# A hybrid decoder step: gate projections of branches D and B ahead of their branch products, kept in DRAM, and two VectorE passes of a triangular inverse in other steps

## Chip, cores and metric

The kernel runs on one core of a Trainium2 chip. The metric is the device time of one execution in microseconds (us), the median of the runs. Engines are named as the profile names them: PE (TensorE matmul), PEld (its weight load), DVE (VectorE), ACT (ScalarE), POOL (GpSimd), SP (SyncE, which here only issues DMAs).

## What is computed

One layer of a decoder for 512 prompt tokens and 8 sample tokens together (520 columns in all). Four branches read one projection of the normed input; each branch output goes through its own matrix and is weighted by a sigmoid gate, and the sum goes on. Cross attention over 256 memory tokens and a convolutional FFN follow. The reference, cut to the part that the change touches:

```python
def token_mixer(xn, p, hist, past):
    z = xn @ p['w_in']
    (a_h, a_b, a_c, g_q, g_k, g_v, g_z, g_a, g_b, c_v, c_g, f_q, f_k, f_v, f_f, gate) = split_cols(z, IN_WIDTHS)
    ...                                            # o_a: short gated conv, o_c: conv + LayerNorm
    o, S = gated_delta_chunked(q, k, v, g_log, beta, hist['gdn'])
    o = rmsnorm(o, p['gdn_norm']) * silu(g_z)      # o_b
    ...
    o_d = forgetting_attention(fq, kk, vv, c[:, -T:], c, q_pos, k_pos)   # the samples: 2048 cached tokens
    gates = sigmoid(gate).reshape(B_, T, N_BRANCH, D_MODEL)
    for i, o_i in enumerate((o_a, o_b, o_c, o_d)):
        merged = merged + gates[:, :, i] * (o_i @ p['w_branch'][i])
    out = merged @ p['w_out']

def gated_delta_chunked(q, k, v, g, beta, s0):     # chunks of C tokens
    A = where(strict, (kb @ k.T) * L, 0) + eye(C)
    sol = triangular_solve(A, concat([v * beta, kb * exp(d)]))
    u, w = sol[..., :DV], sol[..., DV:]
    def step(S, xs):                               # the state goes from chunk to chunk
        v_new = u_i - w_i @ S
        o = qd_i @ S + qk_i @ v_new
        S = S * dl_i + kd_i.T @ v_new
```

## The kernel before

**Pieces.** All large matrix products go through one list, made by `plan`: a *unit* is a block of 256 weight columns, a *piece* is 128 of them, done in two *halves* of 260 tokens. A piece of `w_in` has 8 K tiles, one of `w_branch` 4; each K tile takes three matmuls of 128x260 (high x high, high x low, low x high parts of float32), so a half is 24 or 12 matmuls into `pb`. SP loads a unit two ahead into `raw`; ACT makes the high part `wh` of a piece (L1136), POOL the low part `wl` (L758), each while PE runs the piece before. When a piece is done, ACT (or DVE) takes it out of PSUM (`evac`): for a gate ACT writes tanh into `pairB`, for a branch product DVE multiplies it by that gate and adds it to `xT`.

**Order of pieces.** After the projections of the branches come A's and C's (pieces 44 to 75: two gate pieces, two branch pieces, and so on), then D's (76 to 91), z of branch B (92 to 95, `gz`), B's (96 to 111), then `wo` (112 to 119). A gate is used by the branch piece two pieces later, so two buffers hold all gates.

**Side items.** Everything else is a list `SIDE` of small items. `timeline` puts one item behind each half on PE; each item may have a part on ACT, DVE and PE, in this order, and PE waits for the ACT and DVE parts of an item before its own. The mark `("BEFORE", kind)` says that all items up to it must be out before the first piece of that kind: what has not found a half by then is issued there one after another with no piece between (`through`). Branch B's recurrence is 19 items (`gdn` -1 to 17) for each of four chunks of 128 tokens, every item waiting for the one before; its output norm is the five `gp` items. The mark `("BEFORE", "gateD")` stands behind the four chunks, `gp` and `df`.

**Chunk inverse.** In `gdn` items 2 to 14 the inverse of the unit triangular matrix is built in 7 levels. An even item multiplies `gM` by `gXT` on PE; in the odd item ACT copies that to `gQ`, and PE multiplies it with `gX` from both sides. The DVE part of the next even item then has three passes of 128x512: `gX` += (L1764), the next level's mask into `gM` (L1765, both operands in SBUF), `gXT` += (L1518 of helper `tt`).

**Cached values.** For the samples, 128 pages of `cache_fox_v` (256 KB each) pass through a ring of four buffers in groups of four: `("v", g)` is four PE products of 32x512 that need all four pages; SP loads the next four only when that group is done (`vload`). One half of a group's steps comes with each side item from `VSTART` on; `PAGES` makes the rest come out. After each fourth group ACT, PE and DVE pick rows from the sum (`vsel`); `df` finishes branch D for the samples, from all eight picks.

**Queues.** SP issues unit loads and page loads in the order of the timeline, each behind its own wait. ACT's queue has the stores of small outputs and the loads of the cross attention's memory (`ex` items 0 to 5 store, `ml` items 0 to 3 load `mem_prompt` and the 4 MB of `cache_mem_k`).

## Time and profile before

| | us |
|---|---|
| median of 3 runs | 1886.62 |
| lowest, highest run | 1878.47, 1897.15 |
| the profiled execution | 1892.5 |
| its span in the trace | 1890.7 |
| its mean granted TensorE clock | 0.891 of full |
| busy: PE, PEld, DVE, ACT, POOL | 1581.0, 1446.3, 844.3, 558.6, 633.7 |

Times of stretches below are us from the start of the span. An engine's busy time is the union of its instructions; PE's matmuls are pipelined, so how long a run of matmuls takes is read from start to start. Where a row ends with a bracket, it is the time that the engine sat idle before the row, and what it waited for.

### The profile page before, as it was taken

What the parts mean: (1) busy time and instruction counts of PE and PEld (TensorE: products, weight loads), DVE (VectorE), ACT (ScalarE), POOL (GpSimd) and SP (SyncE); (2) the same over time, 40 slices, a digit from 0 to 9 for tenths busy, and PEclk for the clock granted to TensorE, in tenths of its full rate; (3) what the DMA queues carried; (4) which work ended last, traced back from release to release, by engine and by line L of the source; (5) the groups of instructions that cost most, each with busy time, mean ns of one, the idle gap of its engine ahead of it and who ended that gap; (6) DMA issues with size and microseconds to landing.
All of it is one profiled execution on the core that took longest, in us unless ns stands there. A gap on an engine that the chain in (4) does not pass through costs nothing.

```text
span 1890.7 us, 28588 instructions
## 1 busy us (share of the span) xinstructions
PE 1581.0 (84%) x11204; PEld 1446.3 (76%) x11204; DVE 844.3 (45%) x1320; ACT 558.6 (30%) x907; POOL 633.7 (34%) x354
## 2 busy tenths in 40 slices
PE   7999899876675788866656899898678999999997
PEld 7898787666655787744444899897568899999996
DVE  4106777678796665231211212225332566663001
ACT  4333233343102222110104423334213333333222
POOL 3247344334476752100000243330402344443331
PEclk9999899887678898987776999999868899999998
DMA  6235222142345533443333432233212222222231
GB/s 194 91 113 168 90 90 95 57 128 75 94 131 163 166 102 101 141 124 115 111 111 106 171 101 79 84 129 101 101 67 67 68 90 90 92 98 75 86 113 48
DMA packets 154102, 199.80 MB, mean 106 GB/s; under 512 B 9956, under 2 KB 111901, under 8 KB 153560
## 3 DMA queue, kind: packets, MB, share of 16 engines
q1 hardware_dynamic: 137253, 169.39, 28.3%
q10 hardware_dynamic: 15723, 23.86, 3.7%
q0 software_dynamic: 992, 4.72, 0.8%
q8 instruction: 89, 1.46, 0.3%
q14 instruction: 45, 0.37, 0.1%
HBM read 187.82 MB, written 10.81 MB: 105 GB/s over the span
## 4 chain that ended last, share of the span: by engine, by line
PE 59%; DVE 17%; issue 7%; ACT 7%; DMA 5%; SPq 3%; POOL 1%; ACTq 0%; DVEq 0%; POOLq 0%
PE pb L797 43%; PE sd L797 13%; DMA ar<-in_cache_fox_v 3%; ACT ar L1136 3%; DVE ar L1518 3%; DVE ar L1654 2%; PE sd L801 2%; SPq L671 2%; DVE ar L1538 1%; DVE ar L1661 1%; SPq L672 1%; DVE ar L1521 1%; DVE ar L1524 1%; DMA ar<-in_cache_fox_k 1%; ACT L1136 1%
## 5 line engine op out<-in xcount | busy, mean ns | idle before, releaser
L758 POOL TENSOR_TENSOR wl<-raw,wh 128x1024 fp32r<-128x1024 f32 (+2 forms) x196 | 427.0, 2179 | 1109.2 <-ACT wh L1136 1107.6
L797 PE MATMUL pb<-xh,wh 128*128 128x260 f32 x2176 | 646.9, 297 | 28.0 <-DVE xl L1518 10.3
L797 PE MATMUL pb<-xl,wh 128*128 128x260 f32 x2176 | 630.0, 290 | 0.0
L797 PE MATMUL pb<-xh,wl 128*128 128x260 f32 x2176 | 628.4, 289 | 0.0
L797 PEld LDWEIGHTS pb<-xh,wh 128*128 128x128 f32 x2176 | 425.9, 196 | 45.7 <-issue 35.9
L797 PEld LDWEIGHTS pb<-xl,wh 128*128 128x128 f32 x2176 | 426.9, 196 | 0.7
L797 PEld LDWEIGHTS pb<-xh,wl 128*128 128x128 f32 x2176 | 425.4, 196 | 0.0
L797 PE MATMUL sd<-ar 128*128 128x128 f32 (+7 forms) x1584 | 305.4, 421 | 141.2 <-DVE ar L1518 43.7
L1136 ACT ACTIVATE wh<-raw 128x1024 fp32r<-128x1024 f32 (+2 forms) x208 | 201.6, 969 | 580.7 <-PE pb L797 556.9
L797 PEld LDWEIGHTS sd<-ar 128*128 128x128 f32 (+4 forms) x1584 | 214.6, 216 | 198.7 <-issue 141.0
L769 POOL TENSOR_TENSOR ar<-ar 128x512 f32<-128x512 f32 x128 | 178.6, 1396 | 94.5 <-DMA ar<-in_cache_fox_k 64.3
L797 PE MATMUL pb<-oh,wh 128*128 128x260 f32 (+1 forms) x384 | 118.7, 309 | 12.5 <-DVE wl L1637 4.5
L801 PE MATMUL sd<-cst,ar 128*128 128x128 f32 (+4 forms) x384 | 72.1, 310 | 56.5 <-DVE ar L1518 29.4
L1654 DVE SCALAR_TENSOR_TENSOR ar<-xT,cols,ar 128x512 f32<-128x512 f32 x120 | 114.5, 995 | 1.6
L797 PE MATMUL pb<-ol,wh 128*128 128x260 f32 (+1 forms) x384 | 113.5, 296 | 0.0
L797 PE MATMUL pb<-oh,wl 128*128 128x260 f32 (+1 forms) x384 | 113.4, 295 | 0.0
L1661 DVE TENSOR_REDUCE ar<-ar 128x8 f32<-128x512 f32 x128 | 84.9, 680 | 48.7 <-POOL ar L769 48.1
L797 PE MATMUL sd<-ar,cst 128*128 128x260 f32 (+6 forms) x200 | 63.3, 453 | 51.6 <-DVE ar L1724 19.1
L797 PE MATMUL pb<-hh,wh 128*128 128x260 f32 x352 | 102.1, 290 | 2.6 <-ACT wh L1136 2.6
L1136 ACT ACTIVATE ar<-ar 128x520 f32<-128x520 f32 (+10 forms) x86 | 50.5, 587 | 173.4 <-DVE ar L1544 151.7
L797 PE MATMUL pb<-hl,wh 128*128 128x260 f32 x352 | 100.4, 285 | 0.0
L797 PE MATMUL pb<-hh,wl 128*128 128x260 f32 x352 | 100.2, 285 | 0.0
(173 smaller groups left out, 1678.2 us busy)
## 6 DMA issues: line engine op xcount, KB each, us to landing
raw<-in_w_in SPq DMA_DIRECT2D x40, 1024.0 KB, 5.3
ar<-in_cache_fox_k SPq DMA_DIRECT2D x128, 256.0 KB, 2.7
ar<-in_cache_fox_v SPq DMA_DIRECT2D x128, 256.0 KB, 2.9
raw<-in_w_ffn_in SPq DMA_DIRECT2D x22, 1024.0 KB, 5.0
raw<-in_w_branch SPq DMA_DIRECT2D x16, 512.0 KB, 3.7
raw<-in_w_ffn_out SPq DMA_DIRECT2D x8, 1024.0 KB, 5.1
ar<-in_cache_mem_k ACTq DMA_DIRECT2D x1, 4096.0 KB, 17.4
raw<-in_w_out SPq DMA_DIRECT2D x4, 1024.0 KB, 5.1
```

Of the source, the lines that this page charges most:

```text
L671: n = sp.value_load(ptr_[0:1, i:i + 1], min_val=0, max_val=a[cache].shape[0] - 1)
L672: sp.dma_start(kring[:, i % 4, :], a[cache][bass.ds(n, 1)].rearrange("a p l h d -> (a p) (l h d)"))\
L758: pool.tensor_tensor(wl[:, p % 2, 0:kt, :], raw[:, u % 2, 0:kt, half * P:(half + 1) * P], wh[:, p % 2, 0:kt, :].bitcast(F32), SUB).then_in ...
L769: own(pool.tensor_tensor(kring[:, i % 4, :], kring[:, i % 4, :], qb[:, :], MUL), prod_done)
L797: return pe.matmul(o, l, r, start=start, stop=stop, skip_group_check=True)
L801: return pe.transpose(o, i, ident[0:n, 0:n])
L1136: own(act.activation(o, i, f, **kw), st)
L1518: own(dve.tensor_tensor(o, x, y, op), st)
L1521: own(dve.tensor_scalar(o, x, s1_, s2_, op0, op1) if op1 else dve.tensor_scalar(o, x, s1_, None, op0), st)
L1524: own(dve.scalar_tensor_tensor(out=o, in0=x, scalar=s_, in1=y, op0=op0, op1=op1), st)
L1654: dve_c.by(dve.scalar_tensor_tensor(out=oC[:, c, 0:SEQ], in0=g[:, j - 1:j - 1 + SEQ], scalar=w[:, j - 1:j], in1=oC[:, c, 0:SEQ], op0=MUL, ...
L1661: page_free.by(dve.tensor_reduce(sc[:, i, :], kring[:, i % 4, :].rearrange("p (h d) -> p h d", h=FH), AX, ADD))
```

## The change

The order of pieces becomes: A and C as before (44 to 75), then the eight gate pieces of D (76 to 83), the eight of B (84 to 91), z (92 to 95), then D's eight branch pieces (96 to 103) and B's eight (104 to 111). Sixteen gates no longer wait two pieces but up to twenty for their use, so ACT stores each to DRAM (`gate_scratch`, 266 KB each, on its own DMA queue), and SP loads them back one by one, two pieces ahead of their use, into a ring of four (`pair4`, the memory of both gate buffers). The forced mark moves from the first gate piece of D to the first branch piece of D; `gp` comes behind it, and `("BEFORE", "brB")` is new. z is stored in `oC` and multiplied in at the end of each `gp` item. The split of D's output into high and low parts is now done just ahead of the first branch piece, that of B's just behind B's first half is issued. In the inverse, `gX` += and the mask into `gM` go from the even item to the odd item before it.

```diff
@@ -104,14 +104,19 @@
         unit("w_in", 0, KD, C_AB + h * 256, "ab", 2 * h)
     for n in range(6):
         unit("w_in", 0, KD, C_GQ + n * 256, "gx", 2 * n)
-    for n, br in enumerate("ACDB"):
-        if br == "B":
-            for h in range(2):
-                unit("w_in", 0, KD, C_GZ + h * 256, "gz", 2 * h)
+    for br in "AC":
         b = "ABCD".index(br)
         for h in range(4):
             unit("w_in", 0, KD, C_GATE + b * D + h * 256, "gate" + br, 2 * h)
             unit("w_branch", b * BD, KB, h * 256, "br" + br, 2 * h)
+    for br in "DB":
+        for h in range(4):
+            unit("w_in", 0, KD, C_GATE + "ABCD".index(br) * D + h * 256, "gate" + br, 2 * h)
+    for h in range(2):
+        unit("w_in", 0, KD, C_GZ + h * 256, "gz", 2 * h)
+    for br in "DB":
+        for h in range(4):
+            unit("w_branch", "ABCD".index(br) * BD, KB, h * 256, "br" + br, 2 * h)
     for h in range(4):
         unit("w_out", 0, KD, h * 256, "wo", 2 * h)
     for h in range(4):
@@ -177,8 +182,8 @@
         + [("gdn", n, 0) for n in range(12, 18)]
         + [("dc", n) for n in range(3)] + [("ds", n) for n in range(4)] + [("VSTART",)]
         + [("gdn", n, c) for c in range(1, 4) for n in range(-1, 18)]
-        + [("gp", n) for n in range(5)]
-        + [("PAGES",), ("df", 0)] + [("BEFORE", "gateD")]
+        + [("PAGES",), ("df", 0)] + [("BEFORE", "brD")]
+        + [("gp", n) for n in range(5)] + [("BEFORE", "brB")]
         + [("ex", n) for n in range(6)] + [("ml", n) for n in range(4)] + [("BEFORE", "wo")]
         + [("AFTER", "cq")]
         + [("xm", n) for n in range(3)] + [("x", n) for n in range(XU + 3)] + [("xd", n) for n in range(4)]
@@ -271,7 +276,11 @@
 
     for p in range(NP_):
         kind = PIECES[p][3]
-        if p == first_piece(kind) and ("BEFORE", kind) in SIDE:
+        if kind == "brD" and p == first_piece(kind):
+            evac(p - 2)
+            through(("BEFORE", kind))
+            out.append(("split", "brD"))
+        elif p == first_piece(kind) and ("BEFORE", kind) in SIDE:
             through(("BEFORE", kind))
         if kind in ("wo", "kv", "co", "fg", "fo") and p == first_piece(kind):
             evac(p - 1)
@@ -290,7 +299,7 @@
         for h in range(2):
             at_piece[0] = p - 1 + h
             out.append(("piece", p, h))
-            if kind in ("gateC", "gateB", "gateD") and p == first_piece(kind) and h == 0:
+            if kind in ("gateC", "brB") and p == first_piece(kind) and h == 0:
                 evac(p - 1)
                 out.append(("split", "br" + kind[-1]))
             step(p)
@@ -516,6 +525,8 @@
         sd = ps("sd", [P, 4, 512])
         s0, s1, s2, s3 = (sd[:, n, :] for n in range(4))
 
+        pair4 = v(PR, 4, T)
+        gscr = nc.dram_tensor("gate_scratch", (2, KD, P, T), F32, kind="Internal").ap()
         xscr = nc.dram_tensor("x_scratch", (P, KD * T), F32, kind="Internal").ap()
         qscr = nc.dram_tensor("q_scratch", (NB, 512), F32, kind="Internal").ap()
 
@@ -530,6 +541,7 @@
         qb_in, xs_out, xs_in, qs_out = sem("qb_in"), sem("xs_out"), sem("xs_in"), sem("qs_out")
         out_sem = sem("out_sem")
         stg_out = [sem(f"stg_out{n}") for n in range(2)]
+        gate_out, gate_in = [sem(f"gate_out{n}") for n in range(2)], [sem(f"gate_in{n}") for n in range(4)]
         ss_in, ss_out, mv_in = sem("ss_in"), sem("ss_out"), [sem(f"mv_in{n}") for n in range(2)]
         pool_c, act_c, dve_c = stage("pool_chain"), stage("act_chain"), stage("dve_chain")
         pool_made = stage("pool_made")
@@ -707,10 +719,24 @@
             sp.wait_ge(pt_in, 32)
             for i in range(3):
                 page("cache_fox_k", i)
+            def gate(g):
+
+                if g == 0:
+                    for s in range(2):
+                        sp.wait_ge(gate_out[s], 16 * KD)
+                    sp.wait_ge(ev_all.sem, count(dve_tile, mt_of("gz")))
+                if g >= 4:
+                    sp.wait_ge(mt_dve.sem, mt_d[mt_of("brD", 0) + g - 4])
+                sp.dma_start(pair4[:, g % 4, :], gscr[g // KD, g % KD]).then_inc(gate_in[g % 4], 16)
+
             for e in TIMELINE:
                 if e[0] == "piece" and e[2] == 1 and PIECES[e[1]][1] == 0 and PIECES[e[1]][0] + 2 < len(UNITS):
                     unit(PIECES[e[1]][0] + 2)
-                elif e[0] == "k" and e[1] + 3 < N_PAGE:
+                if e[0] == "piece" and e[2] == 1 and PIECES[e[1]][3] in ("brD", "brB"):
+                    g = e[1] - first_piece("brD")
+                    for i in range(g + 2 if g else 0, min(g + 3, 2 * KD)):
+                        gate(i)
+                if e[0] == "k" and e[1] + 3 < N_PAGE:
                     if e[1] >= 1:
                         sp.wait_ge(page_free.sem, e[1])
                     page("cache_fox_k", e[1] + 3)
@@ -1175,6 +1201,12 @@
                     fn(fs[:, j, :], pb[:, m % 2, 1, TH - NB:TH], ACT.Copy, mt_act, scale=c)
                 elif kind == "cv":
                     fn(both(pairA[:, s, :]), x, ACT.Copy, mt_act, scale=0.5)
+                elif kind in ("gateD", "gateB"):
+                    g = (0 if kind == "gateD" else KD) + idx
+                    if g >= 2:
+                        act.wait_ge(gate_out[s], 16 * (g // 2))
+                    fn(both(pairB[:, s, :]), x, ACT.Tanh, mt_act, scale=0.5)
+                    act.dma_start(gscr[g // KD, idx], pairB[:, s, :]).then_inc(gate_out[s], 16)
                 elif kind == "cg" or kind.startswith("gate"):
                     fn(both(pairB[:, s, :]), x, ACT.Tanh, mt_act, scale=0.5)
                 elif kind in ("gx", "fg"):
@@ -1185,6 +1217,7 @@
                 elif kind == "ac":
                     fn(both(pairA[:, s, :]), x, ACT.Copy, mt_act)
                 elif kind == "gz":
+                    act.wait_ge(gate_out[s], 16 * KD)
                     fn(both(pairA[:, s, :]), x, ACT.Copy, scale=0.5)
                     fn(both(pairB[:, s, :]), x, ACT.Tanh, mt_act, scale=0.5)
                 elif kind == "kv":
@@ -1596,11 +1629,15 @@
                         stt(both(xT[:, idx, :]), both(pairB[:, s, :]), 1.0, x, ADD, MUL, mt_dve)
                         cp(fl8[:, 0:1], fl8[:, 1:2], ev_all)
                     else:
-                        stt(both(tmp), both(pairB[:, s, :]), 1.0, x, ADD, MUL, mt_dve)
+                        g = pairB[:, s, :]
+                        if kind != "brC":
+                            n = (0 if kind == "brD" else KD) + idx
+                            g = pair4[:, n % 4, :]
+                            dve.wait_ge(gate_in[n % 4], 16 * (n // 4 + 1))
+                        stt(both(tmp), both(g), 1.0, x, ADD, MUL, mt_dve)
                         tt(xT[:, idx, :], xT[:, idx, :], tmp, ADD, ev_all)
                 elif kind == "gz":
-                    stt(pairA[:, s, :], pairB[:, s, :], 1.0, pairA[:, s, :], ADD, MUL)
-                    tt(oB[:, idx, :], oB[:, idx, :], pairA[:, s, :], MUL, ev_all)
+                    stt(oC[:, idx, :], pairB[:, s, :], 1.0, pairA[:, s, :], ADD, MUL, ev_all)
                 elif kind in ("wo", "co", "fo"):
                     if kind == "wo" and idx == 0:
                         dve.wait_ge(xs_in, 16)
@@ -1725,7 +1762,8 @@
                             out=t, in0=t, scalar=P ** -0.5 if n <= 2 else 1.0, in1=lrs2[:, j, :], op0=MUL, op1=MUL))
                 elif kind == "gp":
                     dve.wait_ge(a2v.sem, av + 1)
-                    stt(oB[:, n - 1, :], oB[:, n - 1, :], col(V_GN), lrs, MUL, MUL, dve_s)
+                    stt(oB[:, n - 1, :], oB[:, n - 1, :], col(V_GN), lrs, MUL, MUL)
+                    tt(oB[:, n - 1, :], oB[:, n - 1, :], oC[:, n - 1, :], MUL, dve_s)
                 elif kind == "gdn":
                     c = s[2]
                     cc = slice(c * P, (c + 1) * P)
@@ -1758,11 +1796,14 @@
                         dve_s.by(dve.tensor_tensor(gM[:, :, :], gN[:, :, :], lv(1), MUL))
 
                         dve_c.by(dve.tensor_tensor(gQK[:, :, :], gQK[:, :, :], spread(cs(I_UP), GH, 1), MUL))
+                    elif n == 3:
+                        tt(gM[:, :, :], gN[:, :, :], lv(2), MUL, dve_s)
+                    elif n <= 14 and n % 2:
+                        dve_s.by(dve.tensor_tensor(gX[:, :, :], gX[:, :, :], b4(s2), ADD))
+                        if n < 13:
+                            dve_c.by(dve.tensor_tensor(gM[:, :, :], gN[:, :, :], lv((n + 1) // 2), MUL))
                     elif n <= 14:
-                        l = n // 2 - 1
-                        if l < LEVELS - 1:
-                            dve_c.by(dve.tensor_tensor(gX[:, :, :], gX[:, :, :], b4(s2), ADD))
-                            dve_c.by(dve.tensor_tensor(gM[:, :, :], gN[:, :, :], lv(l + 1), MUL))
+                        dve.wait_ge(dve_c.sem, dve_c.n)
                         tt(gXT[:, :, :], gXT[:, :, :], b4(s1), ADD, dve_s)
                     elif n == 17:
                         for h in range(GH):
```

On PE, at the value groups of the second and third chunk: `sd` with 32x512 is a value group, `sd` with 128x128 the products of `gdn` items, `sd<-cst` the pick of rows, `pb` a piece. Before:

```order
L797 MATMUL sd<-ar 32x512 x4
L797 MATMUL sd<-ar 128x128 x12
L797 MATMUL sd<-ar 32x512 x4
L797 MATMUL sd<-ar 128x128 x4
L797 MATMUL sd<-cst,ar 128x8 x4
L797 MATMUL sd<-ar 128x128 x8
L797 MATMUL sd<-ar 32x512 x4
```

The same engine and kind of place after the change:

```order
L823 MATMUL pb<-xl,wh 128x260
L823 MATMUL pb<-xh,wl 128x260
L823 MATMUL sd<-ar 32x512 x4
L823 MATMUL sd<-ar 128x128 x4
L823 MATMUL pb<-xh,wh 128x260
L823 MATMUL pb<-xl,wh 128x260
L823 MATMUL pb<-xh,wl 128x260
```

Where two value groups had twelve products of two items between them and nothing else, each item now stands behind a half of 24 matmuls.

On PE, at the end of the fourth chunk and of the values. Before:

```order
L797 MATMUL sd<-ar 128x128 x12
L797 MATMUL sd<-ar 32x512 x4
L797 MATMUL sd<-ar,cst 128x260 x2
L797 MATMUL sd<-ar 32x512 x4
L797 MATMUL sd<-ar,cst 128x260 x4
L797 MATMUL sd<-ar 32x512 x4
L797 MATMUL sd<-ar,cst 128x260 x2
L797 MATMUL sd<-ar 32x512 x4
L797 MATMUL sd<-cst,ar 128x8 x4
L797 MATMUL pb<-xh,wh 128x260
```

After the change:

```order
L823 MATMUL pb<-xl,wh 128x260
L823 MATMUL pb<-xh,wl 128x260
L823 MATMUL sd<-cst,ar 128x8 x4
L823 MATMUL sd<-ar 128x128 x12
L823 MATMUL sd<-ar 32x512 x16
L823 MATMUL sd<-cst,ar 128x8 x4
L823 MATMUL pb<-oh,wh 128x260
L823 MATMUL pb<-ol,wh 128x260
```

The last four value groups stand together behind the last z piece, and the `gp` items (128x260 with `cst`) are no longer between them; the first piece behind is a branch piece (`oh`).

On DVE, in the inverse of the third chunk before and of the fourth after. Before (L1764 adds to `gX`, L1765 makes the mask, L1518 adds to `gXT`):

```order
L1764 TENSOR_TENSOR ar<-ar,sd 128x512
L1765 TENSOR_TENSOR ar<-ar,cst 128x512
L1518 TENSOR_TENSOR ar<-ar,sd 128x512
L1527 COPY ar<-sd 64x4 x2
L1764 TENSOR_TENSOR ar<-ar,sd 128x512
```

After (L1551 adds to `gXT`, L1802 to `gX`, L1804 makes the mask):

```order
L1551 TENSOR_TENSOR ar<-ar,sd 128x512
L1802 TENSOR_TENSOR ar<-ar,sd 128x512
L1804 TENSOR_TENSOR ar<-ar,cst 128x512
L1560 COPY ar<-sd 64x4 x2
L1551 TENSOR_TENSOR ar<-ar,sd 128x512
```

The passes are the same and as many; L1802 and L1804 now belong to the odd item, and only L1551 to the even one.

## Rows read from the trace of the kernel before

**Rows 1.** The page's first line: the span of the profiled execution.

```profile
span 1890.7 us, 28588 instructions
```

**Rows 2.** Busy time by stretch (PE, PEld, DVE, ACT, POOL), clock, DMA.

```profile
740.00:812.00 72.00, 61.50 (x483) 53.73 (x482) 24.52 (x44) 16.80 (x30) 13.34 (x7) 0.95 0.47 142
812.00:1035.00 223.00, 139.85 (x755) 96.38 (x754) 47.40 (x103) 43.47 (x71) 0.61 (x1) 0.74 0.38 113
...
1072.00:1219.00 147.00, 140.67 (x1162) 139.41 (x1160) 30.48 (x39) 44.05 (x58) 59.71 (x31) 1.00 0.30 94
```

**Rows 3.** Waits in 812 to 1035: who for whom, us, times, longest.

```profile
PE sd L797 <- DMA ar<-in_cache_fox_v: 39.1, 17, 4.8
```

**Rows 4.** PE timeline, two value groups: start, us, tile, count, idle before.

```profile
1021.17 1.57 PE L797 MATMUL sd<-ar 128*32 128x512 f32 x8
...
1029.78 1.93 PE L797 MATMUL sd<-ar 128*32 128x512 f32 x8 [1.43 <-DMA ar<-in_cache_fox_v]
```

**Rows 5.** PE timeline at both ends of pieces 76 to 111.

```profile
814.45 4.11 PE L797 MATMUL sd<-ar 128*128 128x128 f32 x32 [1.33 <-DVE ar L1518]
...
1222.16 0.36 PE L797 MATMUL pb<-xh,wh 128*128 128x260 f32 x1 [3.29 <-DVE xl L1518]
```

**Rows 6.** Chain of work in order of time, in pieces 72 and 73.

```profile
784.22 2.88 PE pb L797 x24
787.10 0.89 PE sd L797 x8
787.99 2.88 PE pb L797 x24
790.87 2.98 PE sd L797 x24
```

**Rows 7.** PE timeline: eight products of item 14, then a half.

```profile
692.06 1.95 PE L797 MATMUL sd<-ar 128*128 128x128 f32 x16
693.77 0.36 PE L797 MATMUL pb<-oh,wh 128*128 128x260 f32 x1
```

**Rows 8.** PE timeline: item 0 of the second chunk, behind a half.

```profile
744.02 1.16 PE L797 MATMUL sd<-ar 128*128 128x128 f32 x8 [1.27 <-ACT ar L1340]
```

**Rows 9.** Line L1765, the mask pass: ns min/median/max, whole run, then 812 to 1035.

```profile
L1765 DVE TENSOR_TENSOR ar<-ar,cst x20: 683/684/2218, 643.5 to 978.2; 128x512 f32<-128x512 f32 x20
...
L1765 DVE TENSOR_TENSOR ar<-ar,cst x10: 684/684/686, 850.1 to 978.2; 128x512 f32<-128x512 f32 x10
```

**Rows 10.** Timelines of POOL, DVE and PE around one long mask pass.

```profile
771.32 2.35 POOL L758 TENSOR_TENSOR wl<-raw,wh 128x1024 fp32r<-128x1024 f32 x1 [6.53 <-ACT wh L1136]
...
771.99 2.22 DVE L1765 TENSOR_TENSOR ar<-ar,cst 128x512 f32<-128x512 f32 x1
...
774.96 2.05 PE L797 MATMUL sd<-ar 128*128 128x128 f32 x8 [4.07 <-DVE ar L1518]
```

**Rows 11.** DVE timeline: `df` behind the last value group, split of D.

```profile
1035.65 2.34 DVE L1518 TENSOR_TENSOR ar<-ar 64x32 f32<-64x32 f32 x6
...
1040.56 2.90 DVE L1518 TENSOR_TENSOR ol<-ar,oh 128x520 fp32r<-128x520 f32 x4 [0.91 <-ACT oh L1136]
```

**Rows 12.** PE timeline: two `gp` items.

```profile
1019.16 2.07 PE L797 MATMUL sd<-ar,cst 128*128 128x260 f32 x4 [5.05 <-DVE ar L1524]
...
1026.28 2.07 PE L797 MATMUL sd<-ar,cst 128*128 128x260 f32 x4 [3.54 <-DVE ar L1524]
```

**Rows 13.** ACT timeline: `ex` items 1 and 5, its last store; PE: `ml` item 2.

```profile
1042.50 0.59 ACT L1136 ACTIVATE ar<-sd 11x512 f32<-11x512 f32 x1
...
1053.75 0.59 ACT L1136 ACTIVATE ar<-sd 38x512 f32<-38x512 f32 x1
1054.37 0.33 ACTq L1227 DMA_DIRECT2D out_cf_p<-ar  x1
...
1066.77 3.52 PE L801 MATMUL sd<-cst,ar 128*128 128x128 f32 x16 [4.65 <-DVE ar L1521]
```

**Rows 14.** The page's DMA issues: count, KB each, median us to landing.

```profile
raw<-in_w_branch SPq DMA_DIRECT2D x16, 512.0 KB, 3.7
```


## What the change does to the time, forecast from these rows

> **What bounds the kernel now.** The page's first line gives the span, 1890.7 us [rows 1]; the execution took 1892.5. PE is busy for 1581.0 of that, so I looked for a stretch where it is not, by busy times in stretches [rows 2]. In 740 to 812 and in 1072 to 1219, where pieces run, PE is busy for 61.50 of 72 and 140.67 of 147 us at a granted clock of 0.95 and 1.00. Between them lie 223 us with PE busy for 139.85 at 0.74, and POOL, which works for pieces alone, busy for 0.61: no piece runs there. That is the forced part ahead of the first gate piece of D: the rest of chunk 1, chunks 2 and 3, `gp`, the value groups from 8 on, `df`. Why PE waits there the wait table tells: 39.1 us in 17 waits for pages of `cache_fox_v` [rows 3]. One group ends at 1021.17 + 1.57 = 1022.74 and the next starts at 1029.78, where PE had waited 1.43 for its page [rows 4]: no two groups can lie closer than 7.04 us, the time in which SP issues four pages and they land. The rest of the idle time belongs to the chain of `gdn` items, each on PE, ACT and DVE in turn. The clock shows in the group itself, 1.93 against 1.57 at other places of the same stretch. So 223 us hold no column of the large products, and the 36 pieces from P76 on come behind them, at nearly full PE use.
>
> **The change part by part.** I rebuild the time from the end of P75 to the first `wo` half, which in the profiled execution starts at 1222.16 behind 3.29 us of waiting for the split of the merged sum [rows 5]; without that wait, 1218.9. From there on nothing changes.
>
> *Start.* By the diff and the order of instructions, P76 no longer stands behind the mark. PE's last products ahead of it are those of item 14 in chunk 1, at 814.45 [rows 5]; eight products cost 1.71 us, 693.77 - 692.06 [rows 7]. P76 starts at 816.2 instead of 1035.
>
> *P76 to P95.* These 20 pieces have 40 halves of 24 matmuls, 2.88 us each [rows 6]: 115.2. Behind each half comes one side item, three chunks' ends and two chunks in all: 236 products at 1.71/8 = 0.214, 50.5. There are 20 value groups; eight products with a group take 2.98 [rows 6], so a group costs 1.27 at this clock, I take 1.2: 24. Four picks of rows, each at most like four products, 0.89 [rows 6]: 3.6. What an item does on ACT and DVE lies beside the next half; item 0 is the exception, its products wait 1.27 behind a half [rows 8], twice: 2.6. The sum is 195.9. The pages stay hidden if two halves and the products of two items last as long as the 7.04: they last 5.76 + 1.7 = 7.5 where items are smallest, and 9.8 on average. The gates' 16 stores go out behind ACT's tanh, and nobody waits for ACT there within a half; I cost them at nothing, and if a whole store were in series with the evac the two buffers still give a piece of 5.8 us for it.
>
> One thing gets worse. The mask pass L1765 lasts 0.684 in all ten cases of 812 to 1035, but up to 2.218 elsewhere [rows 9]. The row of 2.22 began at 771.99, within POOL's split of a weight, 771.32 to 773.67; `gXT` came late, and PE waited 4.07 [rows 10]. POOL idled in 812 to 1035 [rows 2] and will now split one weight per piece in it: 20 × 2.35 = 47 of 198 us, so of passes with both operands in SBUF about one in four meets a split. What is queued behind a long pass is the `gXT` pass in the old order, and PE waits for that; in the new one the mask pass lies in the odd item, with a half more until `gM` is needed, so 1.53 us of stretching is hidden there. Other such passes are in items 1 and 2 and are waited for: I add 2. The Trainium skill says the same of the ports (SBUF — State Buffer, "SBUF: two separate sides"): VectorE with two SBUF inputs against a GpSimd operation that reads SBUF share a pair of ports as an exclusive lock, and the loser blocks for the whole instruction. By that rule every pass that meets a split stretches, which speaks against a plan that brings the splits back; this trace agrees at 771.99, and the rule's worst case is among the rivals. P95 ends at 816.2 + 198 = 1014.
>
> *Tail ahead of the branch pieces.* The order of PE instructions has four value groups back to back. Pick 0.9, twelve products 2.6, the first group 1.2, then three at a cadence of 7.04 + 1.93 (the duration at a low clock, since PE mostly waits): 26.9. `df` starts on DVE at 1035.65, 3.9 behind the end of the last group, 1031.71 [rows 4, 11], and takes 2.5. The split of D, first copy 0.91, then a quarter of 2.90 [rows 11]: 1.6. Together 39.6, to 1053.6. Nothing covers this; SP's loads of the `w_branch` units are early.
>
> *`gp` beside the first five halves of P96 on.* Two such items lie 7.12 apart, on a chain of ACT and DVE [rows 12]; a half of a branch piece has 12 matmuls, 1.44, and cannot hide it. The new multiplication by z adds a pass over 128x520, about 0.7 as the mask pass of nearly that size [rows 9]: 7.8. The first item has no DVE part, 3.2 (a half and as much again, 1.4 to 7.8); then four: 34.5 in all, to 1088.
>
> *`ex` and `ml`.* Items 1 to 5 of `ex` came every (1053.75 - 1042.50)/4 = 2.8 behind halves of 2.88; now behind 1.44. Their own chain is not seen apart: between 1.44 and 2.8, I take 2.6, nearer to the upper row since ACT's copy and PE follow each other: 13, with the first 1.2. The `ml` items took from 1054.37 to the end of a PE part at 1066.77 + 3.52 = 1070.3 [rows 13], on the load of `mem_prompt`: 15.9, as it was. Together 30, to 1118.
>
> *The rest.* P103.1 with its neighbour's end 4.0; the split of B stands exposed, like that of the merged sum 3.3 [rows 5]; P104.0 with what follows the split 3.9; seven more pieces of 2.88, 20.2, which run without gaps as pieces do in 1072 to 1219 [rows 2]. 31.4, so the first `wo` split is due at 1149.6 instead of 1218.9. Eight gate reloads per branch lie on SP's queue two pieces ahead, behind the unit's two loads; a piece is 2.88 and a unit 5.76, a load of `w_branch` lands 3.7 after its issue [rows 14], so I cost them at nothing while the ring of four stays ahead.
>
> *The passes moved, ahead of 812.* In pieces 68 to 75 they take away the wait of 4.07 down to that of item 0's kind, 1.27 [rows 8, 10]: 2.8. Elsewhere before 812 the items lie beside halves or wait for pages of k; bounds +6 and -8, since a collision can move to another pass. I take -3.
>
> Sum: 1149.6 - 1218.9 = -69.3, with -3: -72. On 1892.5 that is 1820.5, and scaled to the median of the three runs (1886.62/1892.5) 1815.
>
> **The rivals.**
>
> *Port lock on what PE waits for.* Not one in four but nearly all of some eight passes of items 1, 2 and `gp` meet a split: 8 × 1.53 = 12, so 1827. For it speaks that POOL's split starts when ACT's `wh` is done, at a fixed place in a piece, so that meetings repeat; against it, that items shift against pieces.
>
> *Gate reloads in series with weights.* A branch unit then needs its weights 3.7 and two gates of 266 KB, each between half of that and all of it by its size, say 2.9, one after another: 9.5 against 5.76, so 8 × 3.7 = 30 and 1845. Against: 1072 to 1219 has loads for the same kind of pieces at a DMA share of only 0.30 [rows 2].
>
> *The clock stays low among the items.* With 0.74 in P76 to P95 instead of near 1, 196 becomes 265, no gain but 4: 1884. Half of it: 1850. Against: 740 to 812 has the same mix of halves and items at 0.95 [rows 2].
>
> *More gain:* `gp` at 1.44 beside branch pieces is faster, or `ex` and `ml` hide: up to 30 less, 1785 to 1800.
>
> *The other side: pages become the bound.* SP now issues pages behind unit loads, whose waits are on POOL and ACT. Should the 7.04 between groups become over 13.4 (9.9 + 72/20), the whole gain is gone, over 14.4 it is a loss of over 1%: 1906. Against: in 740 to 812 unit and page loads already share the queue, with PE busy for 61.50 of 72 [rows 2].
>
> **How the numbers follow.** The forecast with small errors of its terms, 1800 to 1828: 0.62. More gain 0.05, port lock 0.12, reloads 0.09, low clock 0.08, pages 0.04. The range from 1788 leaves out most of "more gain", and to 1848 the low clock and the pages: some 0.16 outside, the rest inside. A measurement of this kernel tells about 1% from no change (the runs span 1878 to 1897). Faster by more than that, under 1868: forecast, gain, lock, reloads and half of the low clock, 0.92. Same: full low clock, 0.04. Slower: pages, 0.04.
>
> **What would show it.** Right: P76 starting near 816; PE busy nearly throughout 816 to 1014 at a clock over 0.95, without waits for `cache_fox_v`; a gap of some 39 us behind P95 with four 32x512 groups 9 us apart; `gp` every 7.8; P104 behind some 3.3 of idle; mask passes of over 2 us without PE waiting for `gXT` behind them. Wrong: branch pieces waiting for `pair4` or weights, long idle times ahead of page groups between pieces, or a clock near 0.74 there.

## The result, and the profile after

The changed kernel took 1820.57 us, the median of four runs (1815.03 to 1829.82), against 1886.40 for the kernel before: a ratio of 0.9652, 95% interval 0.959 to 0.9715. In a second comparison it was 1824.41 us and 0.9688 (0.9662 to 0.9714). The profiled execution took 1815.03; its span, from the page's first line, answers to [rows 1]:

```profile
span 1813.2 us, 28661 instructions
```

Busy times in five stretches of the changed kernel, columns as in [rows 2]: the pieces 76 to 95, the tail behind them, the branch halves P96.0 to P98.1 (with the `gp` items), those up to P103.1 (with `ex` and `ml`), and the split and the pieces of branch B. P96.0 is the first half of piece 96, P96.1 the second.

```profile
804.07:1012.00 207.93, 196.79 (x1603) 176.55 (x1602) 54.37 (x94) 55.92 (x88) 45.14 (x19) 0.98 0.54 167
1012.00:1050.45 38.45, 12.44 (x75) 6.22 (x73) 3.95 (x17) 2.72 (x5) 0.00 (x0) 0.60 0.31 89
1050.45:1082.60 32.15, 20.26 (x88) 18.29 (x88) 8.46 (x13) 22.37 (x28) 4.42 (x3) 0.73 0.26 83
1082.60:1114.60 32.00, 21.60 (x158) 20.10 (x156) 12.43 (x16) 11.29 (x23) 7.74 (x5) 0.84 0.66 233
1114.60:1147.80 33.20, 25.42 (x194) 24.95 (x193) 19.64 (x24) 9.58 (x15) 13.46 (x8) 0.93 0.46 155
```

The 223 us of [rows 2] with PE busy for 139.85 at a granted clock of 0.74 are gone. In their place PE is busy for 196.79 of 207.93 us, at 0.98, and POOL, which had been idle there, works for 45.14. What stays bare is the second row: 38.45 us with PE busy for 12.44, at 0.60.

The timeline of PE, at the places of [rows 4, 5, 12]; the bracket is the idle time before a row:

```profile
802.29 2.02 PE L823 MATMUL sd<-ar 128*128 128x128 f32 x16 [1.33 <-DVE ar L1551]
804.07 0.37 PE L823 MATMUL pb<-xh,wh 128*128 128x260 f32 x1
...
1023.90 1.93 PE L823 MATMUL sd<-ar 128*32 128x512 f32 x8 [7.16 <-DMA ar<-in_cache_fox_v]
1033.02 1.94 PE L823 MATMUL sd<-ar 128*32 128x512 f32 x8 [7.18 <-DMA ar<-in_cache_fox_v]
1042.18 1.94 PE L823 MATMUL sd<-ar 128*32 128x512 f32 x8 [7.22 <-DMA ar<-in_cache_fox_v]
...
1060.67 1.73 PE L823 MATMUL sd<-ar,cst 128*128 128x260 f32 x4 [4.34 <-DVE ar L1551]
...
1068.18 2.07 PE L823 MATMUL sd<-ar,cst 128*128 128x260 f32 x4 [3.37 <-DVE ar L1551]
...
1076.38 2.07 PE L823 MATMUL sd<-ar,cst 128*128 128x260 f32 x4 [4.18 <-DVE ar L1551]
...
1119.08 0.56 PE L823 MATMUL pb<-oh,wh 128*128 128x260 f32 x1 [4.37 <-DVE ol L1551]
...
1147.78 0.56 PE L823 MATMUL pb<-xh,wh 128*128 128x260 f32 x1 [3.42 <-DVE xl L1551]
```

P76 starts at 804.07, directly behind the products of item 14 in chunk 1. The last three value groups lie 9.12 and 9.16 us apart, each behind some 7.2 us of waiting for its pages. `gp` items are 7.5 and 8.2 apart. B's first piece waits 4.37 for its split, and the first `wo` piece starts at 1147.78 instead of 1222.16. What PE waited for in 804 to 1012 (who for whom, us, times, longest), in answer to [rows 3]:

```profile
PE sd L823 <- ACT ar L1373: 4.2, 2, 4.0
PE sd L823 <- DVE ar L1551: 2.5, 2, 1.3
PE sd L823 <- ACT ar L1377: 1.4, 1, 1.4
PE sd L823 <- ACT ar L1375: 1.4, 1, 1.4
PE sd L823 <- DVE ar L1802: 1.3, 1, 1.3
PE sd L823 <- DVE ar L1796: 0.2, 1, 0.2
```

There is no row for `cache_fox_v`: the 39.1 us of waiting for pages have left this stretch. 11.1 us of waiting for ACT and DVE are left.

One sentence on the change ahead of the prediction has to be set right: of the moved passes only the mask goes to the odd item *ahead* of its old place; `gX` += goes from an even item to the odd item *behind* it, since it adds what the odd item before both had multiplied. No term of the sum rests on this.

### The profile page after: what moved, and what is told of

Same layout as the page of the kernel before. It is cut to its first block, busy times and chain, and to the rows that moved or that the text cites. A ratio compares the mean times of both kernels' runs of the same rounds, so it can differ in the third digit from the quotient of the medians.

```text
span 1813.2 us, 28661 instructions
## 1 busy us (share of the span) xinstructions
PE 1541.0 (85%) x11204; PEld 1422.0 (78%) x11204; DVE 860.0 (47%) x1320; ACT 557.3 (31%) x906; POOL 637.6 (35%) x354
## 4 chain that ended last, share of the span: by engine, by line
PE 63%; DVE 18%; ACT 7%; issue 6%; DMA 3%; POOL 2%; SPq 1%; ACTq 0%; DVEq 0%; POOLq 0%
PE pb L823 45%; PE sd L823 15%; ACT ar L1162 3%; DVE ar L1691 3%; DVE ar L1551 2%; PE sd L827 2%; DVE ar L1571 1%; DVE ar L1557 1%; DVE ar L1698 1%; DVE ar L1554 1%; ACT L1162 1%; DMA ar<-in_cache_fox_v 1%; DMA ar<-in_cache_fox_k 1%; POOL ar L795 1%; SPq L683 1%
## 5 line engine op out<-in xcount | busy, mean ns | idle before, releaser
L823 PEld LDWEIGHTS pb<-xh,wh 128*128 128x128 f32 x2176 | 422.7, 194 | 38.9 <-issue 30.4
L823 PE MATMUL sd<-ar 128*128 128x128 f32 (+7 forms) x1584 | 277.4, 378 | 100.6 <-DMA ar<-in_cache_fox_v 24.6
L823 PEld LDWEIGHTS sd<-ar 128*128 128x128 f32 (+4 forms) x1584 | 197.4, 201 | 147.0 <-issue 99.9
L823 PE MATMUL pb<-oh,wh 128*128 128x260 f32 (+1 forms) x384 | 125.6, 327 | 20.9 <-DVE ol L1551 10.6
L823 PE MATMUL pb<-ol,wh 128*128 128x260 f32 (+1 forms) x384 | 117.5, 306 | 0.0
L823 PEld LDWEIGHTS pb<-oh,wh 128*128 128x128 f32 x384 | 81.8, 213 | 28.5 <-issue 27.4
L1557 DVE SCALAR_TENSOR_TENSOR xT<-pb,xT 128x520 f32<-128x520 f32 x24 | 16.8, 699 | 179.9 <-PE pb L823 176.0
```

The source lines that it names most:

```text
L823: return pe.matmul(o, l, r, start=start, stop=stop, skip_group_check=True)
L1557: own(dve.scalar_tensor_tensor(out=o, in0=x, scalar=s_, in1=y, op0=op0, op1=op1), st)
```

## The experiments

**The two VectorE passes alone.** The kernel before with the moved passes and the old order of pieces:

```diff
-        return n in (0, 1, 17) or n <= 14 and n >= 2 and n % 2 == 0
+        return n in (0, 1, 17) or 2 <= n <= 14
...
+                    elif n <= 14 and n % 2:
+                        dve_s.by(dve.tensor_tensor(gX[:, :, :], gX[:, :, :], b4(s2), ADD))
+                        if n < 13:
+                            dve_c.by(dve.tensor_tensor(gM[:, :, :], gN[:, :, :], lv((n + 1) // 2), MUL))
```

> The kernel before with the two VectorE passes moved and the old order of pieces. Theory: the only thing it can take away is PE's wait behind a mask pass that meets POOL's split (4.07 us at 774.96, down to about 1.3), since in 812 to 1035 POOL is idle and no pass is long: 2 to 4 us, ratio 0.998. Rival: the odd item now carries a DVE part that PE waits for, so in the stretch without pieces each odd item gets a wait of its own; 10 such items there by 0.7 us would make it 7 us slower, ratio 1.004.

Measured: 1882.32 against 1887.16 us, ratio 0.998 (0.9955 to 1.0006). The size is as expected, but the interval also holds no change; it does not hold the rival's 1.004. The waits of PE in 740 to 812, of the kernel before and then of this one, show what went:

```profile
PE sd L797 <- DVE ar L1518: 5.4, 3, 4.1
```

```profile
PE sd L797 <- DVE ar L1518: 2.7, 2, 1.3
```

**The order of pieces alone.** The changed kernel with that same edit taken back.

> The changed kernel with the two VectorE passes put back where they were (new order of pieces alone). Theory: POOL splits a weight beside every piece from 76 to 95, so the mask pass in the even items meets one in about one case of four, and PE then waits for the pass behind it: some 10 passes there, 3 to 5 of them by 1.5 to 2.8 us, 5 to 12 us slower than the changed kernel, about 1829, ratio to the kernel before 0.970. Rival: a half of 2.88 us ahead of each item covers the long pass, so no difference from the changed kernel (0.965).

Measured: 1825.06 us, ratio 0.9652 (0.9624 to 0.968), the ratio of the changed kernel itself: the theory's 0.970 was missed, and the rival held. Both were then run on one chip.

> The changed kernel as it is, beside the next one on the same chip: ratio 0.965 to the kernel before.

> The new order of pieces without the moved VectorE passes, beside the changed kernel on the same chip. Theory: the passes stretched by POOL's split are waited for once or twice in pieces 76 to 95, so 2 to 4 us slower than the changed kernel, a ratio 0.001 to 0.002 higher. Rival: no difference that can be told.

Measured: 0.9688 (0.9662 to 0.9714) for the changed kernel, 0.9674 (0.9652 to 0.9695) without the moved passes. The order of pieces is the whole of the gain that can be told; the moved passes are worth less than these intervals. In the profiled executions P76.0 to P95.1 takes 205.0 us in both of the changed kernel, and 207.4 and 206.4 in the two with the order alone, which fits a worth of some 2 us but does not settle it. The stalls that the passes are about are there. In the kernel with the order alone, timelines of POOL, of DVE and of PE around one of them:

```profile
980.02 2.34 POOL L784 TENSOR_TENSOR wl<-raw,wh 128x1024 fp32r<-128x1024 f32 x1 [8.65 <-ACT wh L1162]
```

```profile
980.74 2.17 DVE L1803 TENSOR_TENSOR ar<-ar,cst 128x512 f32<-128x512 f32 x1
982.83 0.67 DVE L1551 TENSOR_TENSOR ar<-ar,sd 128x512 f32<-128x512 f32 x1
```

```profile
983.65 2.05 PE L823 MATMUL sd<-ar 128*128 128x128 f32 x8 [4.01 <-DVE ar L1551]
```

Of its ten mask passes beside pieces 76 to 95 three last 1.68 to 1.77, one 2.17 and two 0.77, but PE waits long for one alone: the others lie beside a half. In the changed kernel the passes are stretched more, and none is waited for. Its DVE timeline:

```profile
883.92 2.22 DVE L1804 TENSOR_TENSOR ar<-ar,cst 128x512 f32<-128x512 f32 x1
...
950.10 2.54 DVE L1804 TENSOR_TENSOR ar<-ar,cst 128x512 f32<-128x512 f32 x1
...
959.74 2.58 DVE L1804 TENSOR_TENSOR ar<-ar,cst 128x512 f32<-128x512 f32 x1
```

Four of the ten passes are over 2.2 us long (984.30 is the fourth; the two of item 3 go through the helper, L1551, and last 0.69), and PE's longest wait behind DVE in this stretch is 1.3.

**Is it POOL's split that stretches them?** In the kernel with the order alone, POOL's splits for pieces 58 to 95 were cut to 16 of 128 columns, which leaves the rest of the low parts as it was:

```diff
+                w_ = 16 if 58 <= p <= 95 else P
-                pool.tensor_tensor(wl[:, p % 2, 0:kt, :], raw[:, u % 2, 0:kt, half * P:(half + 1) * P],
+                pool.tensor_tensor(wl[:, p % 2, 0:kt, 0:w_], raw[:, u % 2, 0:kt, half * P:half * P + w_],
```

> The new order of pieces with the VectorE passes where they were before, in which POOL splits only 16 of 128 columns of the weights of pieces 58 to 95 (the rest of the low part is an old one). Theory: it is POOL's split that stretches the mask passes; with splits of about 0.3 us all ten passes beside pieces 76 to 95 last near 0.684 (before this edit six of ten between 0.77 and 2.17), and PE's wait of 4.0 behind one of them falls to about 1.3. Rival: page DMAs or ACT's reads stretch them, then they stay long.

Measured: one run of 1812.7 us, in which all ten mask passes in 846 to 992 last 0.68 or 0.69. The POOL rows of its groups by line, and the pass that had lasted 2.17:

```profile
L785 POOL TENSOR_TENSOR wl<-raw,wh 128x128 fp32r<-128x128 f32 x19 | 8.7, 460 | 192.8 <-ACT wh L1163 192.8
```

```profile
971.08 0.68 DVE L1804 TENSOR_TENSOR ar<-ar,cst 128x512 f32<-128x512 f32 x1
```

PE's longest wait behind DVE was 2.5 instead of 4.0 (not down to the 1.3 expected). The cause is shown: the split, not the page DMAs, which ran on. With the split ending at 982.36, the long pass above got 0.55 us of its own after it. The Trainium skill (SBUF — State Buffer, "SBUF: two separate sides") says that the loser of the shared port pair blocks fully until the other's instruction is over; the row agrees.

In the rows here it is the one that began later that is longer. In the changed kernel two more mask passes meet a split, at 842.40 and 939.66: the pass begins with the split or ahead of it and lasts 0.69, and it is the split that takes 2.90 and 2.76 instead of 2.4. POOL's timeline:

```profile
842.40 2.90 POOL L784 TENSOR_TENSOR wl<-raw,wh 128x1024 fp32r<-128x1024 f32 x1 [7.11 <-ACT wh L1162]
```

**How much of the stretch were the pages?** In the kernel before, and in the changed one, the pages of groups 8 to 31 were loaded with 16 KB from a fixed place:

```diff
+                        if e[1] >= 8:
+                            sp.dma_start(kring[0:8, i, :], a["cache_fox_v"][0:1].rearrange("a p l h d -> (a p) (l h d)")[0:8])\
+                                .then_inc(page_in[i], 16)
```

> The kernel before, in which the pages of groups 8 to 31 of cache_fox_v are loaded with an eighth of a page from a fixed place (16 KB of 256 KB; no page number is read). The values read by these groups are old ones. Theory: in 812 to 1035 the pages stand on the path in 17 waits of 39.1 us in all; without them the stretch becomes that much shorter, 35 to 39 us, ratio 0.980. Rival: the chain of gdn items is what the stretch is made of and the waits for pages only take the place of waits for ACT and DVE, then 10 to 20 us, ratio 0.992.

Measured: 1844.55 us, ratio 0.9768 (0.9737 to 0.9799): 43 us less. Busy times from 812 to the start of P76, what PE waited for there, and the row of the kernel before for the same DVE line:

```profile
812.00:987.00 175.00, 116.87 (x745) 81.17 (x744) 47.39 (x103) 43.45 (x71) 0.24 (x1) 0.83 0.04 11
```

```profile
PE sd L801 <- DVE ar L1522: 22.6, 14, 2.8
...
PE sd L801 <- DMA ar<-in_cache_fox_v: 1.1, 2, 0.7
```

```profile
PE sd L797 <- DVE ar L1518: 17.7, 11, 2.8
```

The size is the theory's, but the waits alone do not make it. In the profiled executions the stretch is 48.0 us shorter. Waits for pages fall by 38.0, but PE's idle time only by 25.0, from 83.15 to 58.13: the other 13 come back as waits for DVE and ACT, which is the rival's part. The remaining 23.0 are PE's own work, 116.87 instead of 139.85, at a granted clock of 0.83 instead of 0.74. And 175 of the 223 us stay without pages on the path. So of the 83 us of idle time in the old stretch 58 are there without pages too, in the main as waits within the chain of the `gdn` and `gp` items.

> The changed kernel with the same small pages for groups 8 to 31. Theory: pages are hidden behind pieces 76 to 95 and bind only the last three groups behind P95, each of which waits 7.2 us: 18 to 22 us less than the changed kernel, about 1800, ratio 0.954, with pieces 76 to 95 as long as before. Rival: what the page loads take from unit loads or from SP's queue costs time in 76 to 95 as well, then over 25 us less.

Measured: 1807.69 us, ratio 0.9566 (0.9533 to 0.9599), 16 us below the changed kernel of the first comparison if the two ratios are compared; the theory's 18 to 22 counted the whole waits, but a small page also needs time to be issued and to land:

```profile
1025.47 1.94 PE L827 MATMUL sd<-ar 128*32 128x512 f32 x8 [2.76 <-DMA ar<-in_cache_fox_v]
```

From P76.0 to P95.1 it took 204.5 us, from start to start, and the changed kernel 205.0: there the pages cost nothing, neither by themselves nor through SP's queue. From P95.1 to P96.0 it was 28.1 against 41.4.

**Are the stored gates hidden?** The changed kernel without the stores, the loads and the waits for them:

```diff
-                    act.dma_start(gscr[g // KD, idx], pairB[:, s, :]).then_inc(gate_out[s], 16)
...
-                            dve.wait_ge(gate_in[n % 4], 16 * (n // 4 + 1))
```

> The changed kernel without the 16 stores of gates to DRAM and their 16 loads back, and without the waits for them (the branch products are multiplied by whatever stands in the four buffers). Theory: the loads are hidden, no change from the changed kernel, ratio 0.963 to 0.967 to the kernel before. Rival: the loads hold up the weight loads on SP's queue, then up to 30 us less, 0.950.

Measured: 1828.64 us, ratio 0.9702 (0.9676 to 0.9728), which is not faster than the changed kernel and lies within its second comparison: from P76.0 to P112.0 it took 343.6 us, and the changed kernel 343.7. The gates are hidden, but for one. DVE waits for the load of P110's gate, 0.69 us in the first profile of the changed kernel and 1.01 in the second. That decides whether the pass behind it, which adds P110's product to `xT`, begins ahead of POOL's split of a weight (1142.79 in the first) or behind it (1146.46 in the second). DVE's timelines of the two:

```profile
1142.54 0.70 DVE L1551 TENSOR_TENSOR xT<-xT,ar 128x520 f32<-128x520 f32 x1
```

```profile
1146.52 2.87 DVE L1551 TENSOR_TENSOR xT<-xT,ar 128x520 f32<-128x520 f32 x1
```

PE's wait ahead of the first `wo` half is 3.4 in the first and 4.6 in the second, and 3.3 without the gates. So one gate costs at most 1.3 us in these profiles, less than the comparisons can tell.

**The tail: `gp` beside the last pages.**

```diff
+        + [("gp", n) for n in range(5)]
         + [("PAGES",), ("df", 0)] + [("BEFORE", "brD")]
-        + [("gp", n) for n in range(5)] + [("BEFORE", "brB")]
...
-            evac(p - 2)
+            evac(p - 1)
             through(("BEFORE", kind))
```

> The changed kernel with the gp items ahead of the mark for the last pages, so that the gp chain and the last value groups run side by side, as in the kernel before, and the piece of z ahead of the mark is taken out of PSUM before it. Theory: the tail behind P95 is the wait for pages and gp is a chain on ACT and DVE, so they overlap: the tail grows from 38 to about 52 us, the 32 us of gp go, and five halves of 1.4 are left bare at the end: 11 us less than the changed kernel, ratio 0.959. Rival: PE's order makes them wait for each other in turn, then the tail takes 38 + 32 and nothing is won, 0.966 or more.

Measured: 1809.57 us, ratio 0.9596 (0.9574 to 0.9619), as expected in the ratio. The waits for pages and the `gp` chain cover one another (PE timeline):

```profile
1032.75 1.94 PE L823 MATMUL sd<-ar 128*32 128x512 f32 x8 [4.76 <-DMA ar<-in_cache_fox_v]
...
1042.49 2.07 PE L823 MATMUL sd<-ar,cst 128*128 128x260 f32 x4 [5.78 <-DVE ar L1551]
...
1050.34 2.07 PE L823 MATMUL sd<-ar,cst 128*128 128x260 f32 x4 [4.33 <-DVE ar L1551]
1053.31 1.94 PE L823 MATMUL sd<-ar 128*32 128x512 f32 x8 [0.90 <-DMA ar<-in_cache_fox_v]
```

From P95.1 to P96.0 it is 45.3 us instead of 41.4, so the tail grew by 4 and not by the 14 expected, and the 34.5 of the first six branch halves, which had waited for `gp`, become 15.3.

**The tail: all value groups behind pieces.**

```diff
+                if s[0] == "gdn" and s[2] >= 2 and s[1] % 4 == 2:
+                    values()
```

> The changed kernel with one more step of a value group at every fourth gdn item of chunks 2 and 3, so that all 32 groups are issued behind pieces up to P95. Theory: the tail of 38 us loses the three waits of 7.2 and four groups (about 27), pieces 76 to 95 gain four groups of 1.3 and, where two groups come one item apart (5.2 us instead of the 7.04 that pages take), up to 2 us of waiting eight times at most: 10 to 18 us less than the changed kernel, ratio 0.957 to 0.960. Rival: closer pages meet the unit loads on SP's queue and PE waits for pages all along, then no gain.

Measured: 1830.34 us, ratio 0.9706 (0.9686 to 0.9726): no gain over the changed kernel. Here the theory fell, and the result is the rival's. The tail went as expected, from 41.4 to 12.7 us, but P76.0 to P95.1 grew from 205.0 to 239.8. Busy times and waits there:

```profile
810.79:1053.50 242.71, 211.32 (x1632) 184.91 (x1631) 50.76 (x96) 56.40 (x89) 44.10 (x19) 0.93 0.51 157
```

```profile
PE sd L825 <- DMA ar<-in_cache_fox_v: 20.6, 9, 4.0
```

Eight waits of at most 2 us were the bound that I had set; the rows have nine, of up to 4.0, and they make 20.6. PE does not wait for pages all along, as the rival had it. The rest is busy time, 14.5 more, of which four groups are some 5; the others go with the clock, 0.93 instead of 0.98. By these rows a wait in the middle of the stretch cost more than its own length; the clock was not tried by itself.

**The `ml` items later.** From here on with `gp` beside the pages.

```diff
-        + [("ex", n) for n in range(6)] + [("ml", n) for n in range(4)] + [("BEFORE", "wo")]
+        + [("ex", n) for n in range(6)] + [("ml", n) for n in range(2)] + [("AFTER", "brD", 6)]
+        + [("ml", n) for n in range(2, 4)] + [("BEFORE", "wo")]
```

> The kernel with gp beside the last pages, and the last two ml items not before piece 104, so that the load of mem_prompt that they wait for lies beside branch pieces. Theory: the 9.8 us of waiting ahead of that item was in series with branch pieces that did not depend on it; it goes, 8 to 10 us less than with gp beside the pages alone, ratio 0.954 to the kernel before. Rival: the chain of loads of the cross attention behind ml becomes late and the wait reappears in front of its first products, 0.960 again.

Measured: 1810.19 us, 0.9599 (0.9579 to 0.9618), no gain, though the 9.8 us of waiting ahead of `ml` item 2 are gone from their place. They came back in another queue. The chain of work, in order of time:

```profile
1073.64 5.47 DMA ar<-in_mem_prompt
1079.13 1.16 ACT ar L1162 x2
...
1082.06 0.64 ACT wh L1162
...
1084.13 11.41 PE pb L823 x72
```

`ml` item 1 has its own ACT part, which waits for the load of `mem_prompt`; behind it in ACT's queue stand the high parts `wh` of the next weights, and they start at 1082.06, when that part is done. PE waited 7.73 us for them ahead of P101.

```diff
+        + [("ex", n) for n in range(6)] + [("ml", 0)] + [("AFTER", "brD", 4)]
+        + [("ml", n) for n in range(1, 4)] + [("BEFORE", "wo")]
```

> The kernel with gp beside the last pages, in which only ml item 0 (which issues the load of mem_prompt) comes as early as it can, and items 1 to 3 stand behind halves of pieces 102 and 103. Theory: what stopped the version with items 2 and 3 late was item 1, whose ACT part waits for the load with the high parts of the next weights behind it on ACT (PE waited 7.73 us for them); with item 1 late too, that wait is covered by seven halves of 1.4, and 6 to 8 us go: ratio 0.956. Rival: the loads of stored gates (7.3 us in one case where pieces ran close) become the bound and take the gain, 0.960.

Measured: 1803.32 us, ratio 0.9552 (0.9527 to 0.9577), faster than both kernels of this study. PE's wait for `wh` is 1.64 and that ahead of `ml` item 2 3.87 (PE timeline):

```profile
1085.84 0.36 PE L823 MATMUL pb<-oh,wh 128*128 128x260 f32 x1 [1.64 <-ACT wh L1162]
...
1095.71 2.88 PE L827 MATMUL sd<-cst,ar 128*128 128x128 f32 x16 [3.87 <-DVE ar L1554]
```

## Why the prediction was right, point by point

The forecast was 1815 us, and 1820.57 was measured. By stage, in the profiled executions (us; starts read from the timelines):

| | forecast | after |
|---|---|---|
| start of P76 | 816.2 | 804.07 |
| P76 to P95 | 198 | 207.9 |
| tail | 39.6 | 38.5 |
| `gp` beside the first five halves, P96.0 to P98.0 | 34.5 | 30.4 |
| P98.1 to P102.1, with `ex` and `ml` | 30 | 30.2 |
| P103.0 on, with the split of B | 31.4 | 33.3 |
| from P76 on, to the end of P111's evac | 333.4 | 340.3 |

**The start.** 12.1 us early, but only a part of it is the change. At P57 the changed kernel already was 8.8 us ahead (629.14 against 637.94), and both kernels issue the same work up to there; the changed kernel was at 633.1 in a second profile and at 636.1 to 639.3 in two with the order alone. So that part is the spread of executions. The remaining 3.3 stand where I had put the -3 of the moved passes, yet the order alone has 136.6 us from P57 to P72, the changed kernel 136.9 and the kernel before 138.7: whether a pass meets a split there changes from kernel to kernel, and the mechanism is shown, its worth is not.

**P76 to P95.** The step that failed in size. The sum had 193.3 us of work and 4.6 of waiting; the rows have 196.79 and 11.1. The waits that were missing are those for items whose ACT or DVE part is not over when the half is, which I had granted to item 0 alone, with 2 more for stretched passes. Item 0 cost 4.2 instead of 2.6, nearly all in one wait for ACT of 4.0; the old stretch already had that wait (4.0, behind L1340 of the kernel before, which is the same line). Six more waits of 0.2 to 1.4 make up 6.8. Of them only the 0.2 stands behind a stretched pass, in item 2. The 3.5 of work are a matter of the clock: it stood at 0.50 twice, right behind waits, for some 3.4 us each, and at 1.00 else. Windows inside the two:

```profile
927.90:931.20 3.30, 3.30 (x17) 3.30 (x17) 1.65 (x5) 1.37 (x2) 2.38 (x1) 0.50 0.21 81
972.40:975.60 3.20, 3.20 (x17) 3.20 (x16) 1.29 (x2) 1.21 (x2) 0.38 (x1) 0.50 0.48 149
```

What mattered held: PE is busy nearly throughout, pages are hidden (no wait, and no change with small ones), and stretched mask passes are not waited for. One pass in four was to meet a split; six of the ten did, of which four were stretched, and the new places of the passes, or a half beside them, covered them. That every pass that meets a split stretches was more than the rows show: where the pass began first, it was the split that took longer.

**The tail, `gp`, the split of B.** 38.5 for 39.6, three groups at 9.1 for 8.97, `gp` at 7.5 to 8.2 for 7.8, all from rows of the kernel before. But the `gp` term counted one wait too many. The fifth item has no products on PE, so PE waits for three items (7.3, 7.9 and 8.2 us from half to half), not for four, and P98.1 follows P98.0 at once. That is 30.4 instead of 34.5, though the first half took 4.1 instead of 3.2. The split of B cost 4.37 instead of 3.3, and P104 behind it 4.6 instead of 3.9; so the last stage is 1.9 longer than counted.

**The sum.** From P76 to the first `wo` half the gain is 402.7 - 340.3 = 62.4, where 69.3 were forecast; by the medians it is 65.8 in all, where 72 were. That the sum is off by 6.9 and not by 11 is luck: the wait too many at `gp` took back 4.1 of what pieces 76 to 95 and the last stage cost more.

**The rivals.** Gate loads: one of the sixteen is waited for, at up to 1.3 us of PE's time, and without them nothing is won that can be told. Low clock: 0.98. Pages as the bound: not at two halves apart, but the version with closer groups shows that this was near, since 35 us came from one more step at every fourth item. The port lock stretched four of ten mask passes, more than I took, and cost little.

**Why 223 us without pieces could give only 62.** The products and groups of that stretch are work in any order: with small pages 116.87 us of it are PE's, and beside the pieces they still take 207.9 less 40 halves of 2.88, or 92.7. Another 38 us moved into the tail, and 30 of `gp` came behind it, where halves of 1.4 us cover little.

## What to carry to other kernels

A chain of small dependent steps costs little behind large matrix products, so long as a product lasts as long as the step's other engines: put the large pieces where the chain is, rather than ahead of and behind it. What doesn't fit is left over at the end as a tail; let the left-over chains that bind on different things (pages, ACT and DVE) run side by side there, and look for the queue in which a moved wait will stand next. Page groups spaced closer than their loads can follow gave nothing here, and a stretched pass costs nothing until something waits for it.

## What the hardware showed beside

The granted clock fell behind stretches in which PE mostly waited: its mean is 0.60 in the tail, 0.73 in the stretch of `gp` behind it, 0.84 and 0.93 in the next two, against 0.98 in pieces 76 to 95. These means mix two levels, 0.50 (1.2 GHz) and 1.00 (2.4 GHz), and the mean alone misleads: beside `gp` the clock was back at 1.00 before P96.1, and fell again behind each wait, so that from P97.0 on it was mostly low while PE worked and high while it waited. Windows inside three of its steps (PE's busy time is the second number):

```profile
1020.10:1054.10 34.00, 11.34 (x46) 5.97 (x47) 4.49 (x13) 5.17 (x9) 1.39 (x1) 0.50 0.31 92
...
1061.10:1064.40 3.30, 3.30 (x15) 3.02 (x14) 0.00 (x0) 1.92 (x2) 0.55 (x1) 0.50 0.02 9
1064.50:1067.80 3.30, 0.31 (x3) 0.10 (x1) 1.23 (x2) 2.53 (x3) 0.00 (x0) 1.00 0.00 0
```

From its first to its last matmul P96.0 took 2.71 us, P97.0 2.70, P97.1 2.24 and P98.0 2.75, and later halves of the same size 1.32: some 5 us in all.

In the `gp` chain eight ACT table loads take 10.3 us, 1.28 each, in five items:

```profile
L1162 ACT ACT_TABLE_LOAD x8 | 10.3, 1283 | 8.9 <-PE sd L823 8.8
```

They were as many in the kernel before. Two of them stand in the chain of each later item, 2.6 of its 7.8 us; whether another order of ACT's functions would save them was not tried.
